# One-hot quads in neighbouring PSUM bank pairs, with the addition one block earlier on VectorE

## The reference

```python
top_s, top_i = lax.top_k(sc, PEER_TOPK)
...
best_s, best_pos = lax.top_k(cand_s, PEER_TOPK)
idx = jnp.take_along_axis(cand_i, best_pos, axis=-1)
g = jax.nn.softmax(best_s, axis=-1)
u_sel = expert_u[idx]
act = jax.nn.gelu(jnp.einsum('phkd,pd->phk', u_sel, xb), approximate=False)
coef = (g * act.astype(jnp.float32)).astype(xb.dtype)
return jnp.einsum('phk,phkd->pd', coef, expert_v[idx])
```

## Time and profile before

| | us |
|---|---|
| median of 3 runs | 2233.41 |
| lowest, highest run | 2231.43, 2236.27 |
| the profiled execution, its own time | 2236.16 |
| its span, first to last instruction | 2234.8 |
| busy PE, PEld | 2153.6, 1950.2 |
| busy DVE, ACT, POOL | 1620.2, 1005.9, 952.7 |

### The profile page before, as it was taken

One profiled execution on the slowest core, in us unless ns is written; L12 is line 12 of the kernel. 1 busy time (PEld: TensorE's weight loads), 2 busy tenths in 40 slices (PEclk: granted clock), 3 DMA queues, 4 the chain that ended last, 5 costly groups with the idle time before them and its releaser, 6 DMA issues.

```text
span 2234.8 us, 30577 instructions
## 1 busy us (share of the span) xinstructions
PE 2153.6 (96%) x11336; PEld 1950.2 (87%) x11336; DVE 1620.2 (72%) x2857; ACT 1005.9 (45%) x1878; POOL 952.7 (43%) x635
## 2 busy tenths in 40 slices
PE   6999999999999999999999999999999899999998
PEld 3777899999999999999999999988877688888887
DVE  6774579988897897999999999858565475344323
ACT  4433434577777774333333333544554433223221
POOL 0435336777733224656666676443423321111000
PEclk9999999999999999999999999999999999999999
DMA  8646236777779999999999999634242433333332
GB/s 307 194 136 229 92 100 175 202 188 191 196 202 325 346 328 360 375 411 407 410 410 410 407 410 407 213 101 143 72 113 68 147 122 95 96 102 95 100 94 81
DMA packets 195803, 494.96 MB, mean 221 GB/s; under 512 B 33084, under 2 KB 84412, under 8 KB 194944
## 3 DMA queue, kind: packets, MB, share of 16 engines
q1 hardware_dynamic: 131720, 311.51, 41.7%
q0 software_dynamic: 63936, 181.50, 23.1%
HBM read 433.31 MB, written 57.28 MB: 220 GB/s over the span
## 4 chain that ended last, share of the span: by engine, by line
PE 44%; DVE 14%; DMA 10%; issue 3%; ACT 1%; POOL 0%; DVEq 0%; ACTq 0%
PE bank L573 11%; PE bank L577 11%; PE bank L574 11%; DMA scores<-in_rows_v,row_at 6%; DVE scores L2097 4%; DMA scores<-in_rows_u,row_at 3%; DVE scores L2091 3%; DVE weights_lo L1673 3%; DVE hidden L2142 2%; PE bank_stat L949 1%; PE bank_stat L950 1%; PE bank_stat L954 1%; PE bank L994 1%; PE bank L981 1%; PE bank L979 1%
## 5 line engine op out<-in xcount | busy, mean ns | idle before, releaser
L573 PE MATMUL bank<-h_lo,weights_hi 128*128 128x384 f32 (+1 forms) x2148 | 769.8, 358 | 19.4 <-ACT h_hi L1422 7.1
L574 PE MATMUL bank<-h_hi,weights_hi 128*128 128x384 f32 (+1 forms) x2148 | 763.9, 356 | 0.0
L1133 ACT ACTIVATE weights_hi<-weights_raw 128x1024 fp32r<-128x1024 f32 (+1 forms) x411 | 431.8, 1051 | 319.2 <-DMA weights_raw<-in_expert_v 208.7
L1673 DVE TENSOR_TENSOR weights_lo<-weights_raw,weights_hi 128x1024 fp32r<-128x1024 f32 x347 | 438.7, 1265 | 101.3 <-ACT weights_hi L1133 98.7
L577 PE MATMUL bank<-h_hi,weights_lo 128*128 128x384 f32 (+1 forms) x2148 | 458.9, 354 | 0.7 <-DVE weights_lo L1673 0.7
L573 PEld LDWEIGHTS bank<-h_lo,weights_hi 128*128 128x128 f32 x2148 | 407.3, 190 | 55.6 <-ACT h_hi L1422 8.8
L574 PEld LDWEIGHTS bank<-h_hi,weights_hi 128*128 128x128 f32 x2148 | 407.3, 190 | 28.8 <-issue 0.2
L577 PEld LDWEIGHTS bank<-h_hi,weights_lo 128*128 128x128 f32 x2148 | 386.7, 188 | 30.1 <-DVE weights_lo L1673 1.0
L2534 POOL DMA_INDIRECT scores<-in_rows_u,row_at x128 | 171.4, 1339 | 242.1 <-DVE row_coef L2091 188.0
L2484 POOL TENSOR_TENSOR weights_lo<-weights_raw,weights_hi 128x1024 fp32r<-128x1024 f32 x64 | 160.1, 2506 | 238.6 <-ACT weights_hi L1133 238.5
L2547 POOL DMA_INDIRECT expert_coefs<-square x128 | 221.3, 1729 | 91.5 <-issue 45.4
(11 more groups left out here) (461 smaller groups left out, 3343.4 us busy)
## 6 DMA issues: line engine op xcount, KB each, us to landing
weights_raw<-in_expert_u SPq DMA_DIRECT2D x128, 512.0 KB
weights_raw<-in_expert_v SPq DMA_DIRECT2D x128, 512.0 KB
weight<-expert_coefs POOLq DMA_DIRECT2D x32, 768.0 KB
hidden_store<-hidden SPq DMA_DIRECT2D x28, 768.0 KB
hidden<-hidden_store POOLq DMA_DIRECT2D x28, 768.0 KB
expert_coefs<-stage SPq DMA_DIRECT2D x16, 1024.0 KB
ada_raw<-in_w_ada SPq DMA_DIRECT2D x26, 512.0 KB, 6.5
weights_raw<-in_w_ffn_gate SPq DMA_DIRECT2D x22, 512.0 KB
```

Source lines behind the costliest of these rows:

```text
L573: M.matmul(bank[:, 0:width], hi[:, c:c + P], m_lo[k][:, 0:width], start=start and i == 0, stop=False)
L574: M.matmul(bank[:, 0:width], hi[:, c:c + P], m_hi[k][:, 0:width], start=False, stop=False)
L1133: S.activation(w_hi[n % SPLIT][:, 0:w], w_raw[n % RAW][:, 0:w], ACT.Copy).then_inc(*hi_done.inc(n))
L1673: V.tensor_tensor(w_lo[n % SPLIT][:, 0:w], w_raw[n % RAW][:, 0:w], w_hi[n % SPLIT][:, 0:w].bitcast(F32), ALU.subtract).then_inc(*lo_dve.in ...
```

## The change

The seven banks are split: three single banks, and two pairs of neighbouring banks. In the u stage a block, the token transposes and the turned tables take only single banks, a quad takes a whole pair. The pair that was taken longest ago is chosen, so a quad waits for the quad two before it. Everything behind the u stage takes any of the seven, least recently taken first. ACT's copy and DVE's addition of a quad are one operation each over both banks, 512 elements instead of twice 256. DVE adds in block h+2 instead of h+3, and ahead of the row steps of that block; SP stores in block h+3 instead of h+4.

```diff
 class Banks:
-    def take(self, key):
-        self.at[key] = len(self.order) % len(self.tensors)
-        self.order.append(key)
-        return self.tensors[self.at[key]]
...
+    def take(self, key, among):
+        tensor, numbers = min(among, key=lambda choice: max(self.taken.get(n, -1) for n in choice[1]))
+        self.before[key] = [self.owner[n] for n in numbers if n in self.owner]
+        for n in numbers:
+            self.owner[n], self.taken[n] = key, len(self.at)
+        self.at[key] = tensor
+        return tensor
...
-        banks = Banks([ctx.enter_context(nc.psum_tensor(f"bank{i}", [P, T], F32)) for i in range(N_BANKS)])
+        bank_pairs = [ctx.enter_context(nc.psum_tensor(f"bank_pair{i}", [P, 2, T], F32)) for i in range(2)]
+        banks = Banks([ctx.enter_context(nc.psum_tensor(f"bank{i}", [P, T], F32)) for i in range(N_BANKS - 4)], bank_pairs)
...
             def place(tb, quad):
...
-                for half in range(2):
-                    bank = take(("place", tb, quad, half))
-                    for t in range(2):
...
+                pair = take(("place", tb, quad), banks.pairs)
+                for t in range(4):
...
-                hidden_product(j)
+                hidden_product(j, single_banks)
...
             def placed(tb, quad):
...
-                for half in range(2):
-                    S.wait_ge(*pe["place", tb, quad, half])
-                    S.activation(placed_at(tb, quad, half), placed_part(tb, quad, half, 0), ACT.Copy) \
-                        .then_inc(*act.inc(("placed", tb, quad, half)))
+                S.wait_ge(*pe["place", tb, quad])
+                S.activation(placed_at(tb, quad), placed_part(tb, quad, 0), ACT.Copy).then_inc(*act.inc(("placed", tb, quad)))
...
             def placed_quad(tb, quad):
-                for half in range(2):
-                    V.wait_ge(*act["placed", tb, quad, half])
-                    at = placed_at(tb, quad, half)
-                    V.tensor_tensor(at, placed_part(tb, quad, half, 1), at, ALU.add).then_inc(*dve.inc(("place", tb, quad, half)))
+                V.wait_ge(*act["placed", tb, quad])
+                at = placed_at(tb, quad)
+                V.tensor_tensor(at, placed_part(tb, quad, 1), at, ALU.add).then_inc(*dve.inc(("place", tb, quad)))
...
+                for tb, quad in HOT_AT.get(j - 2, ()):
+                    placed_quad(tb, quad)
                 for q in ROW_STEPS.get(("u", j), ()):
                     row_step(q)
-                for tb, quad in HOT_AT.get(j - 3, ()):
-                    placed_quad(tb, quad)
...
-                for tb, quad in HOT_AT.get(j - 4, ()):
+                for tb, quad in HOT_AT.get(j - 3, ()):
                     if 4 * quad % TOK == TOK - 4:
                         store_stage(tb, quad)
```

More of the change, by code:

```diff
@@ L125, with __init__ @@
 class Banks:
-    def __init__(self, tensors):
-        self.tensors, self.order, self.at = tensors, [], {}
-    def take(self, key):
-        self.at[key] = len(self.order) % len(self.tensors)
-        self.order.append(key)
-        return self.tensors[self.at[key]]
-    def before(self, key):
-        n = self.order.index(key) - len(self.tensors)
-        return self.order[n] if n >= 0 else None
+    def __init__(self, singles, pairs):
+        self.tensors = [(bank, (n,)) for n, bank in enumerate(singles)]
+        for i, pair in enumerate(pairs):
+            first = len(singles) + 2 * i
+            self.tensors += [(pair[:, b, :], (first + b,)) for b in range(2)]
+        self.pairs = [(pair, (len(singles) + 2 * i, len(singles) + 2 * i + 1)) for i, pair in enumerate(pairs)]
+        self.at, self.before, self.owner, self.taken = {}, {}, {}, {}
+    def take(self, key, among):
[5 more added lines that the diff above has]
+        return tensor
     def __getitem__(self, key):
-        return self.tensors[self.at[key]]
+        return self.at[key]
 def weight_plan():
@@ L543, in build, with placed_at, placed_part, take @@
         TABLE_AT = 97
[L545 to L551, removed]
+        def placed_at(tb, quad):
+            t0 = 4 * quad
+            return stage[(tb * P + t0) // TOK % 2][:, :, :, t0 % TOK:t0 % TOK + 4].rearrange("p g j t -> p (g j) t")
+        def placed_part(tb, quad, part):
+            return banks["place", tb, quad][:].rearrange("p b x -> p (b x)").rearrange("p (t h n) -> p h n t", t=4, h=2)[:, part]
         def tensor():
             M = nc.tensor
[L557 to L562, removed]
+            def take(key, among=banks.tensors):
+                bank = banks.take(key, among)
+                for before in banks.before[key]:
+                    for done in (act, dve):
+                        if before in done:
+                            M.wait_ge(*done[before])
                 return bank
@@ L583, in tiles_of, with product @@
                 return [m[:, k, :] for k in range(n)]
-            def product(key, n, m_hi, m_lo, ready=None, order=range(KD), at=0, width=T):
-                bank = take(key)
+            def product(key, n, m_hi, m_lo, ready=None, order=range(KD), at=0, width=T, among=banks.tensors):
+                bank = take(key, among)
                 tiles = [(at + k * P, k) for k in order]
@@ L791, in tensor, with hidden_product @@
                         ins.then_inc(*pe.inc(("score", h - 1, c)))
-            def hidden_product(j):
-                product(("u", j), BLOCK_AT["expert_u", j], h_hi_tiles, h_lo_tiles, width=DT)
+            def hidden_product(j, among=banks.tensors):
+                product(("u", j), BLOCK_AT["expert_u", j], h_hi_tiles, h_lo_tiles, width=DT, among=among)
+            single_banks = banks.tensors[0:N_BANKS - 4]
             def own_tokens():
                 for c in range(2):
-                    bank = take(("own_x", c))
+                    bank = take(("own_x", c), single_banks)
                     for k in range(4):
@@ L807, in turn_chosen @@
             def turn_chosen(tb):
-                bank = take(("turn", tb))
+                bank = take(("turn", tb), single_banks)
                 M.wait_ge(*dve["routed", tb])
@@ L816, in place @@
                 tokens, weights = hot[quad % N_HOT][:, 0], hot_weight[quad % N_HOT]
-                for half in range(2):
-                    bank = take(("place", tb, quad, half))
-                    for t in range(2):
[L820 to L823, removed]
+                pair = take(("place", tb, quad), banks.pairs)
+                for t in range(4):
+                    ins = M.matmul(pair[:, t // 2, 256 * (t % 2):256 * (t % 2) + 256], tokens[:, t, :],
+                                   weights[:, t, :, :].rearrange("p h n -> p (h n)"), start=True, stop=True)
+                ins.then_inc(*pe.inc(("place", tb, quad)))
+                pe.also(("place", (tb, quad)), ("place", tb, quad))
             for j in range(AHEAD * GROUP):
@@ L2701, in store_stage @@
                 s = (tb * P + 4 * quad) // TOK
-                Y.wait_ge(*dve["place", tb, quad, 1])
+                Y.wait_ge(*dve["place", tb, quad])
                 Y.dma_start(coefs[:, :, s, :, :].rearrange("g p j t -> p g (j t)"),
```

## The result

The changed kernel takes 2212.91 us (median of 4 runs, 2210.35 to 2217.14) against 2233.97 us before (4 runs, 2231.43 to 2236.27). The ratio of the runs is 0.9917, interval 0.9902 to 0.9932: 18.5 us less, between 15.2 and 21.9. The two medians lie 21.1 us apart, within the same interval. The profiled execution took 2212.41 us, its span is 2211.1 us.

The account below looks back on a forecast made before the run. PE, busy 96% of the span, was taken as the bound. Removing 16.1 us of waits and slow clock gives 2236.2 - 16.1 = 2220.1 us for the profiled execution, 2217.3 us against the median; range 2210 to 2226.

Parts of the forecast that it names:

- Where PE loses time: u stage, blocks 28 to 115: 415.6 us against 392.6 without waits; the 23.0 us excess is nearly all waiting and slow clock.
- All waits on the addition go: u stage: adding a quad one block earlier removes all PE waits on it, 10.9 us for products, 13.1 for loads.
- The size, 16.1 us: u stage: the expected gain from the earlier addition, between bounds of 10.9 and 17.4 us.
- upper bound of 17.4: u stage: the 23.0 us excess less 5.2 for waits on hot_weight and 0.4 for the transposes at block 54.
- 13.1 + 3.0: u stage: 13.1 us of load waits on the addition plus 1.5 us of lost clock in each of two windows.
- Merged operations cost nothing on the path: u stage: one copy and one addition per quad save 3.8 us on each of ACT and DVE, 0 on the path.
- Three banks cost nothing: u stage: a block reuses the bank of the third block before, whose gelu is already done; cost 0.
- DVE's new wait on the copy is covered: u stage: DVE waits up to 1.7 us for ACT's copy, in time it now spends waiting for the high part.
- The gain lasts: Behind the u stage: the mix stage swallows none of the gain, since its transfers start earlier too.
- Rival 1: u stage: DVE becomes the bound through late one-hots or low parts; half the gain goes, 2225 us; chance 0.10.
- Rival 4: u stage: placements wait for one-hot weights at the same moment anyway, so the 16 us stay, 2233; chance 0.04.
- Rivals 2 and 3: u stage, slower: DVE waiting on ACT's copy, 2244, chance 0.05; blocks waiting on a gelu for banks, 2289, chance 0.02.

Follow-up runs that it names:

- the halves: Changed kernel with each copy and each addition split again into two of 256 elements; ratio 0.9926 against the kernel before.
- two banks: Changed kernel with the blocks of the u stage on two of the three single banks; 2214.25 us.
- the addition at once: Changed kernel with the addition one more block earlier (block h+1, store at h+2); 2240.14 us.

## Why the prediction was right

- *Where PE loses time.* Right. The excess of the stretch over 392.6 us was 23.0 us and is 4.3 us now. What is left lies in the blocks with the waits on hot_weight (4.1 us for the loads) and in the block with the transposes.
- *All waits on the addition go.* Right: 10.9 us before, none after, and none in any kernel that adds in block h+2.
- *The size, 16.1 us.* Within the measured 15.2 to 21.9 us, but 2.6 us too low against the stretch (18.7), which even passes the prediction's upper bound of 17.4. Two terms were mis-sized. The first is "13.1 + 3.0": block by block, from the timeline of PE, the ten blocks that waited on the addition were 17.2 us longer than they are now, close to the bound. The two of them with a fall of the clock (PEclk 0.97 in their windows), ended at 463 and 657 us before, were 3.8 us longer than an undisturbed block with a quad; their loads waited 2.2 and 2.1 us, which leaves 1.6 us each where 1.5 was put in for the clock. The other eight were about 0.1 us longer than their loads waited. The second term is the waits on hot_weight, taken as unchanged: their blocks lost 1.5 us less, nearly all of it in block 88, which varies from kernel to kernel, so this part is not shown to come from the change.
- *Merged operations cost nothing on the path.* Right, shown by the halves. The addition takes 0.689 us and the copy 0.580 us; 0.69 and 0.60 were taken from the earlier trace rows.
- *Three banks cost nothing.* Right, shown by two banks. The Trainium skill (Perfetto Trace Analysis, section Matmul Optimizations) asks that all eight PSUM banks be in use, and the prediction read from it that blocks on three banks would lose time. The measurement decides: none was lost in the stretch with three or two, and 0.5 us a block on average (44.8 over 87) with one.
- *DVE's new wait on the copy is covered.* Right in place and bound: 1.6 us at most where 1.7 was worked out, all of it out of idle time.
- *The gain lasts.* Right: the stretch and the ratio agree, so the mix stage gave nothing back.
- *Rival 1* did not come: DVE is busy 394.95 of 447 us, 88%, and no late low part stops PE in the stretch. Rival 4 did not come either: the loads' waits on hot_weight did not grow by what the others shrank (5.2 us before, 4.1 now). Rivals 2 and 3 came only in the kernels made for them, with the addition at once and with one bank.

## What to carry to other kernels

When a consumer that frees a buffer stands at the end of an engine's round, the place of that instruction in the order can be worth more than its duration: count in rounds how far the release stands ahead of the reuse, and move it until it is just behind its own producer, but not past it. Here a wait that was added on DVE cost nothing as long as it replaced idle time that DVE had in the same round; one step further, the same wait stopped PE. For the size of such a gain, compare the stretch with what its rounds take undisturbed, and take off the other causes; the idle times of the waits view leave out the clock and the restart.

## What the runs showed of the hardware

One DVE or ACT operation on float32 that reads across two neighbouring banks took no longer than one of the same size within a bank: from the groups by line and form of the changed kernel (busy us, mean ns):

```profile
L2061 DVE TENSOR_TENSOR stage<-bank_pair,stage 128x512 f32<-128x512 f32 x64 | 44.1, 689 | 19.8 <-ACT stage L1385 18.1
...
L1385 ACT ACTIVATE stage<-bank_pair 128x512 f32<-128x512 f32 x64 | 37.1, 580 | 0.0
```

Against 692 ns and 598 ns for operations of 512 elements from one bank, the crossing shows no cost, which was open in the prediction. With one bank for the blocks, each block of the stretch took 5.0 us whether it placed a quad or not (block 52 apart): 0.9 us more without a quad, 0.4 us more with one.
